# Scores ahead of the turned probabilities: an order change in the attention turns of a two-layer decoder trunk

## The chip, the cores and the metric

The kernel runs on one core of a Trainium2 chip. The metric is the device time of one execution in microseconds (us): the median of three runs is 1085.81 us, the runs lie between 1085.67 and 1086.09. One further execution was recorded by the profiler; all rows below come from it.

The engines are TensorE (PE: matmuls and transposes), VectorE (DVE), ScalarE (ACT), GpSimd (POOL), and SyncE (SP), which only issues transfers. Each runs its own instructions strictly in the order written and waits on semaphores.

## The reference

The input is 512 tokens of width 1024. Two layers follow each other. The first has sliding-window attention with a sink, the second picks 128 keys per query by an indexer and attends to those; both have 16 query heads on 4 key heads of width 64, and both are followed by a squared-ReLU MLP. Cut to what matters here, per block of 128 queries:

```
scores = einsum(q, k) * HEAD_DIM ** -0.5       # one 128-row block of queries
scores = where(valid, scores, -inf)            # window, causal or top-k mask
p = exp(scores - max)                          # softmax, in layer 0 with a sink term
probs = p / sum
out = einsum(probs, v)                         # sums over keys
x = x + rmsnorm(out @ w_out)
```

## The kernel before, in words

All engine streams are written out by hand. Products with the large weights are made as three float32r matmuls (high by high, low by high, high by low); that is the `three`/`dense` pattern of lines 1975 to 1987, called fill below when it stands inside the attention.

The attention of a layer is cut into 16 turns. A turn is one block of 128 queries for four heads. Its work goes through the engines in this order: TensorE makes the scores (`scores`, line 2104: matmuls on 64 rows of the array, two row halves side by side); VectorE masks and scales them into `probs` and finds the maximum (`masked`, line 1435); ScalarE takes the exponential (`expo`, line 1031); VectorE the reciprocal of the sum (line 1442); GpSimd normalises (`normed`, line 779); TensorE transposes each 128x128 block of the probabilities (`transposes`, line 2159, here "turnings": four full-array matmuls against the identity per key block); ScalarE copies the turned block out of its bank (`pt_copy`, line 1038); and TensorE multiplies it with the values (`weighted`, line 2173, here "sums": they write 64 columns of the array at a time).

The turns are pipelined on TensorE. In step n of the loop in `attention` it turns the probabilities of turn n-1, makes the scores of turn n+1, sums turn n-2, turns queries or a new x if the tables `Q_TURN` and `H_TURN` say so (`queries_turned`, line 2084; `new_x`, line 2070), and then does the fill of that step (table `FILL`). Step 9 of the first layer and steps 2 and 5 of the second have no fill. A turn has one or two key blocks in the first layer and one to four in the second. Where the next turn is wider than 256 keys its scores come in two parts, the second behind half of the fill; turnings beyond two blocks also stand there.

What the first instruction of each group waits for:
- scores of turn n+1: the masks of turn n (`s_masked`), because both use the same two banks;
- turnings of turn n-1: the normalised probabilities (`p_done`), and the bank: all turnings, of probabilities, queries and x, go alternately through two banks, and a bank is free when its last user has been copied out (`t_free`);
- sums of turn n-2: the copies (`pt_out`), made a step earlier;
- fill: split weights, and the banks that ScalarE or VectorE has emptied.

ScalarE's stream has in each step: copies of the turned blocks, a half of a weight split in some steps, the high half of turned queries, the exponentials of the next turn, scaled queries or squares of the output, and weight splits. VectorE's has masks, low halves of turned queries, and in the second layer the rounds of the top-k search between all these.

Of the kernel before, what the change touches and what calls it, by code (L numbers as in the profile page):

```python
# [122 lines left out]
TURNS = 16  # L123
# [4 lines left out]
def turn(layer, n):  # L128
    p, i = PAIRS[layer][n // 2]
    return p, i, n % 2  # L130
# [12 lines left out]
def pt_of(layer, n):  # L143
    return range(PT_AT[16 * layer + n], PT_AT[16 * layer + n + 1])
# [34 lines left out]
def q_no(layer, c, j):  # L179


    return 4 * (c - 1) + j if not layer else 7 + 4 * c + j
# [73 lines left out]
def hybrid_trunk(nc, x, x_turned, positions, gains, gains_turned, w_up, w_down, a_in, a_out, sinks, b_in, b_out, consts, out):  # L256
# [4 lines left out]
    with ctx:  # L261
# [305 lines left out]
        def width(layer, i):  # L567
            return len(key_blocks(layer, i)) * P
# [1355 lines left out]
        def _(pe):  # L1924
# [83 lines left out]
            def in_work(layer, s, ks=(0, 1, 2, 3)):  # L2008
                c, h, j = in_step(layer, s)
                u = U[f"in{layer}"] + 2 * c + h  # L2010
                if j == 0 and ks[0] == 0:
                    pe.wait_ge(*low_of(u))
                if c == 0:
                    pe.wait_ge(h_lo, h_no(2 * layer, j, h) + 1)
                ins = dense(u, h, layer, d_no(layer, "in", c, j), in_reg(layer), j, ks)
                if ks[-1] < 3:
                    return
                if h:
                    ins.then_inc(d_done, 1)
                elif j == 3:  # L2020
                    ins.then_inc(first_half_done, 1)
# [24 lines left out]
            def out_work(layer, j, c, h, ks=(0, 1, 2, 3)):  # L2046
                u = U[f"out{layer}"] + 2 * c + h
                if ks[0] == 0:
                    if j == 0:
                        pe.wait_ge(*low_of(u))  # L2050
                    if h == 0 and c == 0:
                        pe.wait_ge(o_lo_done, 8 * layer + max(pair_of(layer, p, j) for p in range(2)) + 1)
                ins = dense(u, h, layer, d_no(layer, "out", c, j), q_reg(layer), j, ks)
                if ks[-1] < 3:
                    return
                if h:
                    ins.then_inc(d_done, 1)
                elif j == 3:
                    ins.then_inc(first_half_done, 1)

            def new_x(norm, j):

                layer = norm // 2
                pe.wait_ge(x_new, 8 * (norm - 1) + 2 * j + 2)
                for h in range(2):
                    bank = t_free(layer, ("h", norm, j, h))
                    if norm == 2 and j == 0:
                        pe.wait_ge(tile_out, LAYER_TILES - 4)
                    for k in range(4):
                        ins = nc.tensor.transpose(bank[:, blk(k)], X[:, j, blk(4 * h + k)], ident[:, 0:P])  # L2070
                    ins.then_inc(h_t, 1)
# [8 lines left out]
            def queries_turned(layer, qn):  # L2080
                bank = t_free(layer, ("q", qn))
                pe.wait_ge(q_roped, qn + 1)
                for r in range(4):
                    ins = nc.tensor.transpose(bank[:, blk(r)], qs[:, qn % 2, blk(r)], ident[:, 0:P])
                ins.then_inc(q_t, 1)
# [42 lines left out]
            def scores(layer, n, rr):  # L2128
                N = 16 * layer + n
                p, i, rh = turn(layer, n)  # L2130
                W, k0 = width(layer, i), key_blocks(layer, i)[0] * P
                if rr == 0:
                    pe.wait_ge(k_lo_done, 4 * layer + i + 1)
                    pe.wait_ge(q_lo_done, q_no(layer, p + 1, i) + 1)
                    if N:
                        pe.wait_ge(s_masked, 4 * N)
                    else:
                        pe.wait_ge(kv_out, 4)
                elif W > 256:
                    pe.wait_ge(s_masked, 4 * N + 2)  # L2140
                qh, ql = q_reg(layer)
                c0 = 256 * rr if W <= 256 else 0
                pairs = []
                for a in range(2):
                    rows = slice(64 * a, 64 * a + 64)
                    t = 4 * p + 2 * rh + rr
                    pairs.append((banks[s_bank(layer, a)][:, c0:c0 + W], qh[rows, t, blk(i)], ql[rows, t, blk(i)],
                                  k_hi[rows, p, k0:k0 + W], k_lo[rows, p, k0:k0 + W]))
                for ins in by_rows(pairs):
                    ins.then_inc(s_ready, 1)  # L2150

            def transposes(layer, n, c):
                N = 16 * layer + n
                K = PT_AT[N] + c
                bank = t_free(layer, ("pt", K))
                if c == 0:
                    pe.wait_ge(p_done, 4 * N + 4)
                for e in range(4):
                    ins = nc.tensor.transpose(bank[:, blk(e)], probs[:, N % 3, e, blk(c)], ident[:, 0:P])
                ins.then_inc(pt_ready, 1)  # L2160
# [17 lines left out]
            def attention(layer):  # L2178
                norm = 2 * layer + 1

                def fill(s, ks=(0, 1, 2, 3)):
                    if s < FILL_OUT[layer]:
                        in_work(layer, FILL_IN[layer] + s, ks)
                    else:
                        m = s - FILL_OUT[layer]
                        out_work(layer, m // 4, m % 4 // 2, m % 2, ks)

                def turned(n):
                    for c, j in Q_TURN[layer].get(n, ()):
                        queries_turned(layer, q_no(layer, c, j))  # L2190
                    for j in H_TURN[layer].get(n, ()):
                        new_x(norm, j)

                def scores_of(n):
                    scores(layer, n, 0)
                    if width(layer, turn(layer, n)[1]) <= 256:
                        scores(layer, n, 1)

                for n in (-1, 0):
                    steps = FILL[layer].get(n, ())  # L2200
                    for s in steps[:1]:
                        fill(s)
                    if n == -1:
                        turned(n)
                        for s in steps[1:]:
                            fill(s)
                    scores_of(n + 1)
                    if n == 0:
                        turned(n)
                        for s in steps[1:]:  # L2210
                            fill(s)
                for n in range(1, TURNS + 2):
                    turning = len(pt_of(layer, n - 1)) if n - 1 < TURNS else 0
                    summing = len(pt_of(layer, n - 2)) if n >= 2 else 0
                    wide = n + 1 < TURNS and width(layer, turn(layer, n + 1)[1]) > 256
                    second = wide or turning > 2 or summing > 2
                    for c in range(min(turning, 2)):
                        transposes(layer, n - 1, c)
                    if n + 1 < TURNS:
                        scores_of(n + 1)  # L2220
                    for c in range(min(summing, 2)):
                        weighted(layer, n - 2, c)
                    turned(n)
                    steps = FILL[layer].get(n, ())
                    for s in steps[:-1]:
                        fill(s)
                    if steps:
                        fill(steps[-1], (0, 1) if second else (0, 1, 2, 3))
                    if second:
                        for c in range(2, turning):  # L2230
                            transposes(layer, n - 1, c)
                        if wide:
                            scores(layer, n + 1, 1)
                        for c in range(2, summing):
                            weighted(layer, n - 2, c)
                        if steps:
                            fill(steps[-1], (2, 3))
# [142 lines left out]
            for s in range(8, 12):  # L2380
                in_work(0, s)
                keys_turned(0, s - 8)
            attention(0)
            out_tail(0)
            mlp(0)
# [37 lines left out]
            for s in range(8, 20):  # L2423
# [5 lines left out]
                if s in (16, 17):  # L2429
                    queries_turned(1, s - 3)  # L2430
            pe.wait_ge(idx_relu, 24)
            attention(1)
            out_tail(1)
            mlp(1)
# [36 lines left out]
```

## Time and profile before

| what | us |
|---|---|
| median of three runs | 1085.81 |
| profiled execution | 1088.47 |
| its span, first to last instruction | 1086.7 |
| TensorE busy | 1055.2 (97%) |
| VectorE busy | 744.4 (68%) |
| ScalarE busy | 540.4 (50%) |
| GpSimd busy | 184.7 (17%) |

The profiled execution took 1088.47 us, of which 1.8 us lie outside its span; it is 2.7 us longer than the median of the runs. TensorE is busy 97% of the span. The attention of the first layer runs from about 55 to 165 us of the span, that of the second from about 611 to 728 us. Start times in rows are us from the start of the span. A matmul's recorded length overlaps that of the next, so the time that TensorE gives to a group is read from the start of its first to the start of the next group's first.

### The profile page before, as it was taken

Reading aid. Unit: us, or ns where it says so; the run is one execution under the profiler, and the core shown is the slowest. Engines: PE = TensorE matmul, PEld = TensorE weight load, DVE = VectorE, ACT = ScalarE, POOL = GpSimd, SP = SyncE. Lnnn points to the kernel's source line nnn. Section 1 sums busy time; section 2 is a strip of 40 time slices with the busy share of each in tenths; the row PEclk is TensorE's granted clock in tenths of the full one; section 3 lists DMA queues with packets and bytes.
Section 4 is the critical chain, followed back from the end, with each engine's and each line's share of the span. In section 5 each row is a group of like instructions: output and inputs, shape, how many; then the busy total and the mean of one; then the engine's idle time right before and its main releaser. Section 6 shows DMA issues by size and latency. Waiting matters only on the chain. (4 is left out here: it accounts for less than half of the span.)

```text
span 1086.7 us, 14782 instructions
## 1 busy us (share of the span) xinstructions
PE 1055.2 (97%) x5372; PEld 856.3 (79%) x5372; DVE 744.4 (68%) x1283; ACT 540.4 (50%) x1018; POOL 184.7 (17%) x330
## 2 busy tenths in 40 slices
PE   7899999999999999999999989999999999999997
PEld 6677678988888888888777766679888888888885
DVE  4364644587698697687678898536586697696684
ACT  6486753454445444425554576645353453453431
POOL 1345420000000000005412377430000000000004
PEclk9899999999999999999999999999999999999999
DMA  9431505634454455432523333005644535535502
GB/s 293 117 79 40 118 1 114 139 78 109 85 114 110 87 114 111 86 78 50 117 59 78 78 77 80 1 1 119 134 92 102 111 84 116 110 84 117 110 8 78
DMA packets 52009, 99.94 MB, mean 92 GB/s; under 512 B 4704, under 2 KB 4832, under 8 KB 51936
## 3 DMA queue, kind: packets, MB, share of 16 engines
q1 hardware_dynamic: 51360, 98.87, 40.4%
q8 instruction: 43, 0.70, 0.3%
q14 instruction: 30, 0.25, 0.1%
q10 hardware_dynamic: 576, 0.11, 0.1%
HBM read 96.88 MB, written 2.10 MB: 91 GB/s over the span
## 5 line engine op out<-in xcount | busy, mean ns | idle before, releaser
L1975 PE MATMUL bank<-r_hi,w_hi 128*128 128x512 f32 (+1 forms) x456 | 177.5, 389 | 0.0
L1976 PE MATMUL bank<-r_hi,w_lo 128*128 128x512 f32 (+1 forms) x456 | 177.4, 389 | 0.0
L1977 PE MATMUL bank<-r_lo,w_hi 128*128 128x512 f32 (+1 forms) x456 | 177.4, 389 | 0.0
L1583 DVE TENSOR_TENSOR w_lo<-w_raw,w_hi 128x1024 fp32r<-128x1024 f32 x84 | 102.1, 1223 | 70.5 <-ACT w_hi L1123 70.4
L1123 ACT ACTIVATE w_hi<-w_raw 128x1024 fp32r<-128x1024 f32 x84 | 87.9, 1056 | 119.5 <-PE bank L1977 82.9
L2314 PE MATMUL bank<-w_hi,hid_hi 128*128 128x512 f32 x336 | 130.7, 389 | 0.0
L2315 PE MATMUL bank<-w_lo,hid_hi 128*128 128x512 f32 x336 | 130.7, 389 | 0.0
L2316 PE MATMUL bank<-w_hi,hid_lo 128*128 128x512 f32 x336 | 130.7, 389 | 0.0
L1132 ACT ACTIVATE w_hi<-w_raw,gT 128x512 fp32r<-128x512 f32 x96 | 64.5, 716 | 106.5 <-DMA w_raw<-in_w_mlp_up 75.1
L787 POOL TENSOR_TENSOR acc<-acc,G 128x512 f32<-128x512 f32 x8 | 13.0, 1650 | 594.3 <-ACT waste L983 594.3
L1977 PEld LDWEIGHTS bank<-r_lo,w_hi 128*128 128x128 f32 (+1 forms) x456 | 85.2, 187 | 18.2
L1975 PEld LDWEIGHTS bank<-r_hi,w_hi 128*128 128x128 f32 (+1 forms) x456 | 85.2, 187 | 18.0
L1976 PEld LDWEIGHTS bank<-r_hi,w_lo 128*128 128x128 f32 (+1 forms) x456 | 85.2, 187 | 18.0
L779 POOL TENSOR_TENSOR probs<-probs,small 128x256 f32<-128x256 f32 (+3 forms) x128 | 78.1, 641 | 89.6 <-DVE small L1442 89.4
L1985 PE MATMUL bank<-w_hi,r_hi 128*128 128x512 f32 x208 | 86.5, 416 | 1.4 <-issue 0.6
L1664 DVE SCALAR_TENSOR_TENSOR w_lo<-w_raw,gT,w_hi 128x512 fp32r<-128x512 f32 x96 | 68.3, 747 | 27.6 <-ACT w_hi L1132 27.6
L1987 PE MATMUL bank<-w_hi,r_lo 128*128 128x512 f32 x208 | 82.0, 394 | 0.0
L1986 PE MATMUL bank<-w_lo,r_hi 128*128 128x512 f32 x208 | 81.6, 392 | 0.0
L1031 ACT ACTIVATE probs<-probs,small 128x257 f32<-128x257 f32 (+5 forms) x128 | 65.4, 516 | 25.1 <-DVE small L1435 25.0
L2315 PEld LDWEIGHTS bank<-w_lo,hid_hi 128*128 128x128 f32 x336 | 63.1, 188 | 13.1
L2316 PEld LDWEIGHTS bank<-w_hi,hid_lo 128*128 128x128 f32 x336 | 63.1, 188 | 13.1
L2314 PEld LDWEIGHTS bank<-w_hi,hid_hi 128*128 128x128 f32 x336 | 63.1, 188 | 13.1
(200 smaller groups left out, 2143.1 us busy)
## 6 DMA issues: line engine op xcount, KB each, us to landing
w_raw<-in_w_mlp_up SPq DMA_DIRECT2D x64, 512.0 KB, 6.5
w_raw<-in_w_mlp_down SPq DMA_DIRECT2D x64, 512.0 KB, 6.9
w_raw<-in_b_w_in SPq DMA_DIRECT2D x16, 512.0 KB, 6.9
w_raw<-in_a_w_in SPq DMA_DIRECT2D x8, 512.0 KB, 8.7
w_raw<-in_a_w_out SPq DMA_DIRECT2D x8, 512.0 KB, 5.7
w_raw<-in_b_w_out SPq DMA_DIRECT2D x8, 512.0 KB, 6.6
xt<-in_x_turned SPq DMA_DIRECT2D x8, 256.0 KB, 6.3
w_raw<-in_a_w_in SPq DMA_DIRECT2D x8, 256.0 KB, 6.5
```

The source lines that it names most:

```text
L779: nc.gpsimd.tensor_tensor(v, v, inv_sum[:, N % 3, c:c + 1].to_broadcast([P, W]), ALU.mult).then_inc(p_done, 1)
L1123: nc.scalar.activation(half_of(w_hi[:, u % 2, :], a), b_of(name, a), ACT.Copy).then_inc(b_hi_done, 1)
L1583: nc.vector.tensor_tensor(half_of(w_lo[:, u % 2, :], a), b_of(PRODUCTS[i][1], a), half_of(w_hi[:, u % 2, :], a).bitcast(f32), ALU.subtract ...
L1975: nc.tensor.matmul(bank, whi, xhi, start=start, stop=False)
L1976: nc.tensor.matmul(bank, wlo, xhi, start=False, stop=False)
L1977: return nc.tensor.matmul(bank, whi, xlo, start=False, stop=stop)
L1985: nc.tensor.matmul(bank[:], xh, hi[:, k, :], start=h == 0 and k == 0, stop=False)
L1986: nc.tensor.matmul(bank[:], xh, lo[:, k, :], start=False, stop=False)
L1987: ins = nc.tensor.matmul(bank[:], xl, hi[:, k, :], start=False, stop=h == 1 and k == 3)
L2314: nc.tensor.matmul(bank[:], xh[:, k, blk(j)], hi[:, k, :], start=k == 0, stop=False)
L2315: nc.tensor.matmul(bank[:], xh[:, k, blk(j)], lo[:, k, :], start=False, stop=False)
L2316: ins = nc.tensor.matmul(bank[:], xl[:, k, blk(j)], hi[:, k, :], start=False, stop=k == 3)
```

## The change

In each step n from 1 to 14 the scores of turn n+1 are issued ahead of the first two blocks' turnings of turn n-1; before, they stood behind them. Step 15 and later have no scores. Nothing is added or removed, and the streams of the other four engines are the same.

```
--- before.py
+++ after.py
@@ -2214,10 +2214,10 @@
                     summing = len(pt_of(layer, n - 2)) if n >= 2 else 0
                     wide = n + 1 < TURNS and width(layer, turn(layer, n + 1)[1]) > 256
                     second = wide or turning > 2 or summing > 2
+                    if n + 1 < TURNS:
+                        scores_of(n + 1)
                     for c in range(min(turning, 2)):
                         transposes(layer, n - 1, c)
-                    if n + 1 < TURNS:
-                        scores_of(n + 1)
                     for c in range(min(summing, 2)):
                         weighted(layer, n - 2, c)
                     turned(n)
```

TensorE, first layer, step 6, before: the end of the last fill (`w_hi`, `r_lo`), the turnings of two key blocks (`probs`), the scores of turn 7 (`k_hi`, `k_lo`), the sums (`pt`) and four query turnings (`qs`).

```order
L1987 MATMUL bank<-w_hi,r_lo 128x512
L2159 MATMUL bank<-ident,probs 128x128 x8
L2104 MATMUL bank<-k_hi,r_hi 128x128 x2
L2104 MATMUL bank<-k_hi,r_lo 128x128 x2
L2104 MATMUL bank<-k_lo,r_hi 128x128 x2
L2104 MATMUL bank<-k_hi,r_hi 128x128 x2
L2104 MATMUL bank<-k_hi,r_lo 128x128 x2
L2104 MATMUL bank<-k_lo,r_hi 128x128 x2
L2173 MATMUL bank<-pt,kvs 64x256 x4
L2084 MATMUL bank<-ident,qs 128x128 x4
```

The same place of TensorE with the change:

```order
L1987 MATMUL bank<-w_hi,r_lo 128x512
L2104 MATMUL bank<-k_hi,r_hi 128x128 x2
L2104 MATMUL bank<-k_hi,r_lo 128x128 x2
L2104 MATMUL bank<-k_lo,r_hi 128x128 x2
L2104 MATMUL bank<-k_hi,r_hi 128x128 x2
L2104 MATMUL bank<-k_hi,r_lo 128x128 x2
L2104 MATMUL bank<-k_lo,r_hi 128x128 x2
L2159 MATMUL bank<-ident,probs 128x128 x8
L2173 MATMUL bank<-pt,kvs 64x256 x4
L2084 MATMUL bank<-ident,qs 128x128 x4
```

The eight turnings moved from ahead of the twelve score matmuls to behind them, next to the sums.

TensorE, second layer, steps 5 and 6, as a difference: there is no fill between the steps, so the turnings of turn 5 (the row with the minus) followed the query turnings of step 5 at once.

```order
 L2104 MATMUL bank<-k_lo,r_hi 128x256 x2
+L2159 MATMUL bank<-ident,probs 128x128 x8
 L2173 MATMUL bank<-pt,kvs 64x256 x2
 L2084 MATMUL bank<-ident,qs 128x128 x4
-L2159 MATMUL bank<-ident,probs 128x128 x8
 L2104 MATMUL bank<-k_hi,r_hi 128x256 x2
 L2104 MATMUL bank<-k_hi,r_lo 128x256 x2
```

The row with the plus is turn 4's, moved behind the scores of turn 6. With the change the scores of turn 7 follow the query turnings.

## Rows read from the trace of the kernel before

**Rows 1.** Windows: length; busy PE, PEld, DVE, ACT, POOL; granted clock; DMA
```profile
55.00:165.00 110.00, 106.83 (x712) 82.27 (x711) 59.40 (x185) 74.27 (x204) 47.42 (x104) 1.00 0.25 58
611.00:728.00 117.00, 109.15 (x717) 76.47 (x716) 82.95 (x243) 78.20 (x205) 64.66 (x91) 0.99 0.17 38
628.00:631.00 3.00, 3.00 (x9) 2.27 (x8) 2.93 (x12) 1.44 (x6) 3.00 (x7) 0.50 0.01 3
```

**Rows 2.** TensorE's timeline, first layer, step 4 (start, length, instruction, idle before)
```profile
78.35 0.39 PE L1987 MATMUL bank<-w_hi,r_lo 128*128 128x512 f32 x1
78.59 1.03 PE L2159 MATMUL bank<-ident,probs 128*128 128x128 f32 x8
79.55 0.39 PE L2104 MATMUL bank<-k_hi,r_hi 64*128 64x256 f32 x2
...
80.45 1.08 PE L2173 MATMUL bank<-pt,kvs 128*64 128x256 f32 x8
```

**Rows 3.** TensorE's timeline, places that price a change of kind
```profile
59.31 0.39 PE L1987 MATMUL bank<-w_hi,r_lo 128*128 128x512 f32 x1
59.63 0.33 PE L2104 MATMUL bank<-k_hi,r_hi 64*128 64x128 f32 x2
...
63.29 0.60 PE L2159 MATMUL bank<-ident,probs 128*128 128x128 f32 x4
63.82 0.39 PE L2104 MATMUL bank<-k_hi,r_hi 64*128 64x256 f32 x2
...
64.73 0.66 PE L2084 MATMUL bank<-ident,qs 128*128 128x128 f32 x4
65.14 0.48 PE L1985 MATMUL bank<-w_hi,r_hi 128*128 128x512 f32 x1
...
590.01 0.60 PE L2084 MATMUL bank<-ident,qs 128*128 128x128 f32 x4
590.37 0.48 PE L1985 MATMUL bank<-w_hi,r_hi 128*128 128x512 f32 x1
```

**Rows 4.** A turning and its first copy, TensorE and ScalarE, step 3
```profile
73.26 1.03 PE L2159 MATMUL bank<-ident,probs 128*128 128x128 f32 x8
...
73.89 1.09 ACT L1038 ACTIVATE pt<-bank 128x512 f32<-128x512 f32 x2 [0.32 <-PE bank L2159]
```

**Rows 5.** First layer, steps 9 and 10, TensorE and ScalarE
```profile
107.62 1.03 PE L2159 MATMUL bank<-ident,probs 128*128 128x128 f32 x8
...
108.41 1.07 ACT L1038 ACTIVATE pt<-bank 128x512 f32<-128x512 f32 x2
...
115.21 0.66 PE L2084 MATMUL bank<-ident,qs 128*128 128x128 f32 x4 [1.62 <-ACT pt L1038]
```

**Rows 6.** Second layer, step 3, TensorE, and VectorE's last mask before it
```profile
625.67 0.63 PE L2159 MATMUL bank<-ident,probs 128*128 128x128 f32 x4 [1.69 <-POOL probs L779]
626.44 0.38 PE L2104 MATMUL bank<-k_hi,r_hi 64*128 64x256 f32 x2
...
625.93 0.35 DVE L1435 CUSTOM_DVE_ANT_0 probs<-bank,band,small 128x128 f32<-128x128 f32 x1
```

**Rows 7.** Second layer, steps 5 to 8, TensorE and ScalarE
```profile
637.24 1.03 PE L2159 MATMUL bank<-ident,probs 128*128 128x128 f32 x8
...
638.97 1.07 ACT L1038 ACTIVATE pt<-bank 128x512 f32<-128x512 f32 x2
...
642.25 0.66 PE L2159 MATMUL bank<-ident,probs 128*128 128x128 f32 x4 [1.47 <-DVE r_lo L1376]
...
645.40 0.66 PE L2084 MATMUL bank<-ident,qs 128*128 128x128 f32 x4 [0.56 <-ACT pt L1038]
...
662.97 0.45 PE L2104 MATMUL bank<-k_hi,r_hi 64*128 64x384 f32 x2 [1.73 <-DVE small L1435]
```

**Rows 8.** Second layer, step 9, VectorE and TensorE
```profile
664.89 0.61 DVE L1435 CUSTOM_DVE_ANT_0 probs<-bank,score,small 128x384 f32<-128x384 f32 x1
...
665.19 1.04 PE L2159 MATMUL bank<-ident,probs 128*128 128x128 f32 x8
```

More of the change, by code:

```diff
@@ L2216, in attention @@
                     second = wide or turning > 2 or summing > 2
+                    if n + 1 < TURNS:
+                        scores_of(n + 1)
                     for c in range(min(turning, 2)):
                         transposes(layer, n - 1, c)
-                    if n + 1 < TURNS:
-                        scores_of(n + 1)
                     for c in range(min(summing, 2)):
```

## The prediction, made before the changed kernel was run

> **What bounds the kernel.** I read the table of busy time first: TensorE is busy 97% of the span, so what counts is the time that TensorE gives to its groups, and its waits. Then the windows over the two attentions [rows 1]: TensorE is busy 106.83 of 110 us in the first and 109.15 of 117 us in the second. There are 3.2 and 7.9 us of idle time, and nothing else in the kernel is touched by the change. VectorE (83.0 us) and ScalarE (78.2 us) are far from full in the second, but both work in a fixed order, so a late item delays what stands behind it. Last I read the timelines of TensorE at each wait, with the engine that ended it.
>
> No work is added. The sum has two kinds of terms: what another order of matmul kinds costs TensorE, and what each wait becomes.
>
> **Changes of kind.** Fill and turnings use the whole array, scores use it in two row halves, sums in two column halves. In a usual step before [rows 2] the last fill starts at 78.35, turnings follow 0.24 later, scores 0.96 after those (eight turnings), sums 0.90 after those: 2.10 us from the last fill to the sums. In the new order: fill to scores takes 0.32 (59.31 to 59.63) [rows 3]; scores to the next whole-array group 0.91 (63.82 to 64.73) [rows 3]; then the turnings, up to a group of another kind, 0.96 as before [rows 2]; and four turnings that stand behind scores take 0.41 where four behind fill take 0.36 [rows 3], so 0.05 more. Sum 2.24, that is about 0.15 us more per step. It is one more change of kind: fill, turnings | scores | sums | fill has three, fill | scores | turnings | sums | fill has four. Turnings followed by sums have no row here; I take them like turnings followed by scores, 0.53 for four (63.29 to 63.82) [rows 3]. If that change were free the term would be 0.06, if it cost twice as much 0.24.
>
> The Trainium skill, page "TensorEngine Tiling (Array Packing)", section "Key Properties", says that changing the tiling mode drains TensorE. It gives no price. By that rule alone the new order has one drain more in each step, which speaks against the change; whoever counts matmuls alone finds nothing.
>
> Of the 14 steps of a layer that have scores, step 1 has no sums and as many changes as before. So 13 steps, 26 in both layers: 3.9 us if TensorE never waited. The waits alter this, layer by layer.
>
> **First layer.** Steps 2 to 8 add 7 x 0.15 = 1.05, of which step 8 gives back about 0.15, since its query turning waits for GpSimd, whose work follows the fill. So TensorE reaches step 9 about 0.9 late. There the turnings started at 107.62 and ScalarE's copies at 108.41 [rows 5]. In the new order they start at 107.62 + 0.9 + 0.08 (fill to scores instead of turnings) + 0.91 (scores) = 109.51. A copy can begin 0.63 after the first turning (73.26 to 73.89, where ScalarE stood idle for it) [rows 4], with the 0.05 above 0.68: 110.19, that is 1.78 us later than 108.41. From that copy on ScalarE has no gap before (half a weight split, four exponentials, the output's high half, another split) until the copy which the query turnings of step 10 wait for; they start at 115.21 after 1.62 idle [rows 5]. All of it moves by 1.78, so these start at about 116.99. TensorE's own lateness is hidden in that wait; 0.8 us come on top. The copy that sets it is late because it now stands behind scores. Step 11's 0.15 is given back at a wait for split weights that hang on the same ScalarE chain. Steps 12 to 14 add 0.45. First layer: 1.78 + 0.45 = 2.2 us. In the other query steps (2, 4, 6) the copy had over 1.4 us in hand, and the new order takes about 1.0.
>
> **Second layer.** Here VectorE's top-k rounds set the pace of the masks. In step 3 TensorE waited 1.69 us for the probabilities, turned them (625.67) and started the scores at 626.44; the last mask began at 625.93 and took 0.35, so it ended at 626.28 [rows 6]. The scores can't go earlier, since the masks hang on VectorE's rounds and not on TensorE. In the new order TensorE waits for the masks, starts the scores at 626.44 as before, and the four turnings that lay inside the wait stand behind them: 0.53 + 0.05 = 0.58 us late [rows 3]. This replaces what steps 1 to 3 would add; in steps 1 and 2 the same happens on a smaller scale and is hidden at 626.44.
>
> Steps 4 and 5 add 0.15 each. Step 5's turnings start at 637.24 + 0.73 + 0.08 + 0.91 = 638.96, and their copy at 639.64 instead of 638.97 [rows 7]: 0.7 late. From there ScalarE goes without a gap to the high half of the queries, VectorE then makes the low half, and this ended the 1.47 us before the second block's turnings at 642.25 [rows 7]. In step 6 the scores now fill that wait. So TensorE would gain up to 0.9 us, but it gains nothing: ScalarE's chain, 0.7 late, goes on to the copy that releases the query turnings at 645.40, and VectorE's chain to the masks that release the second part of the scores at 662.97 after 1.73 us idle [rows 7]. Both move by 0.7. What TensorE wins in between it waits there. At 662.97 the second layer is 0.7 late.
>
> In step 9 the turnings started at 665.19; the last mask began at 664.89 and took 0.61, so it ended at 665.50 [rows 8]. The scores, now first, are ready at 665.19 + 0.7 + 0.08 = 665.97 but must wait for the masks at 665.50 + 0.7 plus a few hundredths, 666.25. That costs 0.28 besides the 0.15: 1.1 late. Step 10's 0.15 goes into a wait of 0.5 for the output's low half. Steps 11 to 14 add 0.6: 1.7 us.
>
> **Sum.** 2.2 + 1.7 = 3.9 us. The profiled execution of 1088.47 would become 1092.4. It lies 2.7 above the median of the runs, and I carry the difference over: 1085.8 + 3.9 = 1089.7 us. That the sum equals 26 x 0.15 is chance: waits give some back and two chains add.
>
> **Rivals.**
> 1. Scores fill the waits of the turnings, and it gets faster. The waits ended by probabilities, or by the bank of a query turning, are 1.69, 1.47 and two of 0.41 and 0.25. Scores (0.9) in their place would save 0.9 + 0.9 + 0.41 + 0.25 = 2.5 us; with masks 0.9 earlier, up to 0.9 of the 1.73 at 662.97 too. With free changes of kind the time is 1082.4 to 1083.3, with 3.9 for them still 1086.3. It decides as soon as a turn's masks are done when the turnings would have started. Against it: at 626.44 the scores were released by the masks and not by the turnings [rows 6], and the wait at 662.97 ends with VectorE's rounds.
> 2. Nothing: changes of kind are hidden by weight loads and the chains have more slack than I read. 1085.8, with one chain late 1086.6. Against it are the two pairs 0.24 / 0.32 and 0.36 / 0.41 [rows 2, 3].
> 3. The clock. From 628 to 631 TensorE had half its clock, 1.2 GHz instead of 2.4 (0.50) [rows 1], after the idle time of step 3; the fill there took about twice its time, so such a stretch of 3 us costs some 1.5 us. The new order makes single waits longer: about 2.1 us in step 3 and some 2.4 us ahead of the query turnings of step 10 in the first layer, where 1.62 left the clock alone. One such stretch more gives 1091.2. If the one in the second layer fell where TensorE waits anyway, 1088.2.
>
> That the order does not change can be left out: the streams show it.
>
> **How the numbers follow.** Of this kernel a difference of about 0.2%, 2.2 us, can be told from none. Forecast as worked out: 0.63, 1087.9 to 1091.0 by itself (changes of kind at 0.08 a step below, a chain later by a us above). Rival 3 with a slower clock: 0.17. Rival 2: 0.13. Rival 1: 0.07, of which I put 0.04 at faster and the rest within 0.2%. Slower by over 0.2% (over 1088.0) holds most of the first and all of the slower clock: 0.80. Within 0.2%: 0.16. Faster: 0.04. The range that leaves out 2 in 10 is 1086.9 to 1091.7.
>
> **What would show it right or wrong.** In the trace after, scores follow fill by 0.32 and turnings follow scores with a first step longer by 0.05; from the last fill to the sums 2.24 instead of 2.10. The query turnings of step 10 in the first layer still wait for ScalarE's copy and start near 117.0. The scores of step 3 in the second layer start no earlier than before, and the turnings behind them. TensorE's idle time in both windows changes by under 1.5 us, though its work takes longer. I am wrong if fill to sums takes 2.1, if the wait at 662.97 shrinks, or if the masks run ahead of TensorE in steps 1 to 9 of the second layer.

## The result and the profile after

The changed kernel takes 1090.31 us (median of 11 executions, 1086.6 to 1092.5); the kernel before, on the same chip, takes 1085.67 us (11 executions). The ratio is 1.0042 with a 95% interval of 1.0029 to 1.0054, that is 3.1 to 5.9 us slower. The profiled execution took 1090.9 us, its span 1089.1 us.

Spans of the two profiles differ by 2.4 us only, because they differ by 2.5 us of the other sign before the change begins. In the start-up, at about 34 us, TensorE waited 4.60 us for VectorE and then ran at half clock for 6.8 us in the profile of before, against 3.25 and 3.4 us in that of after. So I compare start times with those of the same instruction before, and count from the first attention's fill (56.71 before, 54.22 after). By that measure the first layer costs 3.7 us and the second 1.2.

The windows of after (length; busy PE, PEld, DVE, ACT, POOL; granted clock; DMA), to be held against [rows 1]:

```profile
55.00:165.00 110.00, 106.49 (x688) 79.56 (x687) 58.50 (x181) 72.25 (x201) 47.50 (x104) 0.98 0.26 58
611.00:728.00 117.00, 110.59 (x705) 76.11 (x705) 83.98 (x246) 78.08 (x204) 65.83 (x94) 0.97 0.18 40
116.00:119.00 3.00, 3.00 (x9) 2.33 (x8) 2.65 (x2) 2.27 (x9) 0.00 (x0) 0.50 0.98 203
628.00:631.00 3.00, 3.00 (x19) 1.80 (x16) 2.86 (x10) 1.16 (x4) 3.00 (x7) 0.50 0.02 5
648.50:651.50 3.00, 2.98 (x7) 2.42 (x8) 2.90 (x11) 1.60 (x7) 3.00 (x5) 0.50 0.67 177
```

TensorE's idle time has hardly changed (3.5 us of 110 instead of 3.2; 6.4 of 117 instead of 7.9). The first layer has a stretch at half clock (0.50, so 1.2 GHz) that it did not have before, at 116. The second has a further one at 648.5.

A usual step, TensorE, first layer, step 4 of after, against [rows 2]:

```profile
76.13 0.39 PE L1987 MATMUL bank<-w_hi,r_lo 128*128 128x512 f32 x1
76.45 0.38 PE L2104 MATMUL bank<-k_hi,r_hi 64*128 64x256 f32 x2
...
77.35 1.09 PE L2159 MATMUL bank<-ident,probs 128*128 128x128 f32 x8
78.37 1.08 PE L2173 MATMUL bank<-pt,kvs 128*64 128x256 f32 x8
```

Fill to scores takes 0.32, scores to turnings 0.90, turnings to sums 1.02: 2.24 us from the last fill to the sums, where it was 2.10. From the fill of one step to that of the next, steps 3, 5 and 7 each add 0.13 to 0.16.

Steps 9 and 10 of the first layer, TensorE and then ScalarE, against [rows 5]:

```profile
106.95 1.09 PE L2159 MATMUL bank<-ident,probs 128*128 128x128 f32 x8
109.05 0.39 PE L2104 MATMUL bank<-k_hi,r_hi 64*128 64x256 f32 x2 [0.42 <-DVE small L1435]
114.45 0.66 PE L2084 MATMUL bank<-ident,qs 128*128 128x128 f32 x4 [2.38 <-ACT pt L1038]
```

```profile
107.64 1.08 ACT L1038 ACTIVATE pt<-bank 128x512 f32<-128x512 f32 x2 [0.80 <-PE bank L2159]
108.61 1.92 ACT L930 ACTIVATE w_hi<-w_raw 128x2048 fp32r<-128x2048 f32 x1
113.81 1.08 ACT L1038 ACTIVATE pt<-bank 128x512 f32<-128x512 f32 x2
```

With the 2.49 us added by which after is ahead, the turnings of step 9 start at 109.44, their copies at 110.13 (1.72 later than before) and the query turnings at 116.94 (1.73 later), behind a wait of 2.38 instead of 1.62. ScalarE now stands idle for TensorE at 107.64. The 0.42 at 109.05 is new: scores of turn 11 wait for the masks of turn 10, whose scores went out only 3.00 us earlier.

The second layer of after, first TensorE against [rows 6] and [rows 7], then ScalarE:

```profile
627.60 0.41 PE L2104 MATMUL bank<-k_hi,r_hi 64*128 64x256 f32 x2 [1.87 <-DVE small L1435]
644.09 0.66 PE L2159 MATMUL bank<-ident,probs 128*128 128x128 f32 x4 [0.27 <-DVE r_lo L1376]
647.23 0.66 PE L2084 MATMUL bank<-ident,qs 128*128 128x128 f32 x4 [1.47 <-ACT pt L1038]
664.23 0.44 PE L2104 MATMUL bank<-k_hi,r_hi 64*128 64x384 f32 x2 [0.24 <-DVE small L1435]
666.92 0.44 PE L2104 MATMUL bank<-k_hi,r_hi 64*128 64x384 f32 x2 [0.31 <-DVE small L1435]
```

```profile
640.80 1.08 ACT L1038 ACTIVATE pt<-bank 128x512 f32<-128x512 f32 x2
646.57 1.09 ACT L1038 ACTIVATE pt<-bank 128x512 f32<-128x512 f32 x2
655.25 1.06 ACT L914 ACTIVATE r_hi<-w_raw 128x1024 fp32r<-128x1024 f32 x1 [2.67 <-DMA w_raw<-in_b_w_out]
```

This layer begins 1.16 us later on its profile's time scale than before, which is the 3.65 us that the first layer left less the 2.49. The scores of step 3 are 1.16 late too, so the change has not moved them by itself. The query turnings are 1.83 late (0.67 more), and their wait has grown from 0.56 to 1.47 while that of the second block's turnings shrank from 1.47 to 0.27: most of what was won in the one was waited in the other. At 664.23 (662.97 before) it is 1.26, so 0.10 more than at the start and not the 0.7 forecast, and the wait there shrank from 1.73 to 0.24. At the layer's end it is 2.39.

### The profile page after: what moved, and what is told of

Its sections match the earlier page's. It is cut to its first block and busy times, and to the rows that moved or that the text cites. A ratio compares the mean times of both kernels' runs of the same rounds, so it can differ in the third digit from the quotient of the medians.

```text
span 1089.1 us, 14782 instructions
## 1 busy us (share of the span) xinstructions
PE 1059.9 (97%) x5372; PEld 856.0 (79%) x5372; DVE 743.9 (68%) x1283; ACT 541.4 (50%) x1018; POOL 185.0 (17%) x330
```

## The experiments

Each changes `attention`; where a condition is named, the steps outside it keep the order of before:

```
first = <condition>
if first and n + 1 < TURNS:
    scores_of(n + 1)
for c in range(min(turning, 2)):
    transposes(layer, n - 1, c)
if not first and n + 1 < TURNS:
    scores_of(n + 1)
```

**The first layer alone.** `first = layer == 0`.

> The scores stand first in the steps of the first layer alone. Kinds and chains: 26 changes of kind are halved (13 x 0.15 = 2.0 us), and the copies of step 9 come 1.8 us late, so the query turnings of step 10 start 1.8 later than before measured from the start of the attention, and the first layer ends 2.1 us later; the second layer adds nothing. Time +2.1 us against the kernel before, or +3.7 where a stretch at half clock follows the longer wait of step 10. Kinds alone, without chains: query turnings of step 10 no later than before, +0.5 from the steps after them. Second layer as the only cause: 0.

Measured: ratio 1.0019 (1.0007 to 1.0031). In its profile the query turnings of step 10 are 1.73 late behind a wait of 2.38, a half-clock stretch follows, and the layer ends 3.7 late. The second layer, unchanged, returned 0.75 of it; the table below says why.

**The second layer alone.** `first = layer == 1`.

> The scores stand first in the steps of the second layer alone. Kinds and chains: first layer as before with 1.62 us of wait in step 10; scores of steps 1 to 3 of the second layer at the same distance as before, sums 0.6 later, query turnings of step 6 0.7 later; the layer ends 1.2 us later (as in the profile of the change) to 1.8 us later (if the weight load between steps 6 and 8 takes as long as before). Time +1.2 to +1.8 us. Kinds alone: +2.0 from 13 steps. The clock as the only cause: 0.

Measured: 1.0007 (0.9997 to 1.0017), which can't be told from no change. In the profile the first layer is as before and the second costs 1.22, as it does in after. The ratios of the two halves add up to 1.0026, with the one for both at 1.0042. With intervals of 0.001 to each side these times don't contradict a plain sum, but they don't show one closely either.

**Step 9 of the first layer alone.** `first = (layer, n) == (0, 9)`. Is it the late copy that sets the query turnings of step 10?

> The scores stand first in step 9 of the first layer and nowhere else. Chain theory: step 9's turnings start 1.0 later, the copies 0.9 later (108.41 becomes 109.3), and the query turnings of step 10 start 0.9 later, though TensorE idles before them: +0.9 us, a bit less where the wait for split weights gives back. Rival, only changes of kind cost: 0.15 go into the wait of 1.62 us: 0.0 us.

TensorE and then ScalarE in that kernel, which is 2.37 us ahead of before at this place:

```profile
106.27 1.09 PE L2159 MATMUL bank<-ident,probs 128*128 128x128 f32 x8
113.76 0.66 PE L2084 MATMUL bank<-ident,qs 128*128 128x128 f32 x4 [2.74 <-ACT pt L1038]
```

```profile
106.96 1.09 ACT L1038 ACTIVATE pt<-bank 128x512 f32<-128x512 f32 x2 [0.80 <-PE bank L2159]
113.12 1.08 ACT L1038 ACTIVATE pt<-bank 128x512 f32<-128x512 f32 x2
```

The copies are 0.92 late, the query turnings 0.92, and 0.93 is what is left at the layer's end. The chain through ScalarE is shown: one step's order, with no work added and TensorE idle behind it, costs its whole delay. The ratio is 1.0007 (0.9994 to 1.0020), too wide to tell 0.9 us by itself: this rests on the profile. The wait of 2.74 was followed by no half-clock stretch.

**All but that step.** `first = (layer, n) != (0, 9)`.

> The change as it is, but step 9 of the first layer keeps the old order. Chain theory: TensorE comes to step 9 0.9 us late, the turnings and the copies are 0.9 late (not 1.8), so the query turnings of step 10 start 0.9 later than before, with a wait of about 1.6 us as before and so without a stretch at half clock behind it; the first layer ends 0.9 + 0.45 = 1.35 later instead of 2.15. Time about 0.8 us below the changed kernel, 2.4 below where that one has the half clock. Kinds alone: 0.15 below the changed kernel.

TensorE at steps 9 and 10:

```profile
110.83 0.39 PE L2104 MATMUL bank<-k_hi,r_hi 64*128 64x256 f32 x2 [1.45 <-DVE small L1435]
...
114.45 0.66 PE L2084 MATMUL bank<-ident,qs 128*128 128x128 f32 x4 [0.60 <-ACT pt L1038]
```

The query turnings are 0.83 late, what steps 2 to 8 had gathered, and the layer ends 1.15 late. That is 0.9 less than the 2.05 of the changed kernel where its clock holds (its third profile, below), and 2.5 less than the 3.7 where it doesn't. I had expected a wait of 1.6 ahead of the query turnings; it is 0.60, because the waiting moved to the scores (1.45, for masks), which changes nothing in the sum. Ratio 1.0014 (1.0003 to 1.0026).

**Three changes of kind instead of four.** Scores, sums, turnings: the turned block is summed a step later anyway, so the sums may stand between.

```
 if n + 1 < TURNS:
     scores_of(n + 1)
+for c in range(min(summing, 2)):
+    weighted(layer, n - 2, c)
 for c in range(min(turning, 2)):
     transposes(layer, n - 1, c)
-for c in range(min(summing, 2)):
-    weighted(layer, n - 2, c)
```

> Order scores, sums, turnings, so there are three changes of kind as before (fill | scores | sums | turnings, fill), with scores still first and turnings later by the sums as well. If the 0.15 us per step is the price of the fourth change, a step without query turnings (step 3, 5 or 7 of the first layer) takes as long from fill to fill as before. The copies come another 0.6 to 1.1 us later than with the change: the query turnings of step 10 in the first layer start 2.3 to 2.8 us later than before less the 0.9 that the kinds cost there, and those of steps 4 and 6 now follow turnings at once and wait 0.3 us for a copy. Time +2 to +3 us in all. If scores first is what costs and not the change of kind, steps 3, 5, 7 are 0.15 longer and time is over +4 us.

TensorE in step 4 and, last, the query turnings of step 10:

```profile
76.00 0.39 PE L1987 MATMUL bank<-w_hi,r_lo 128*128 128x512 f32 x1
76.31 0.38 PE L2104 MATMUL bank<-k_hi,r_hi 64*128 64x256 f32 x2
...
77.22 1.08 PE L2173 MATMUL bank<-pt,kvs 128*64 128x256 f32 x8
78.23 1.09 PE L2159 MATMUL bank<-ident,probs 128*128 128x128 f32 x8
...
115.35 0.66 PE L2084 MATMUL bank<-ident,qs 128*128 128x128 f32 x4 [2.96 <-ACT pt L1038]
```

From the fill of one step to the next, steps 3, 5 and 7 now take 0.02 to 0.05 less than before: the 0.15 is gone with the fourth change of kind, though the scores still stand first. So it is the price of the change of kind. The Trainium skill says in "TensorEngine Tiling (Array Packing)", "Key Properties", that changing the tiling mode drains TensorE. The traces agree as far as they go: they show a cost, 0.15 us for one change more per step, and not the drain itself.

For the total the expectation of 2 to 3 us missed by far: ratio 1.0067 (1.0055 to 1.0079), some 7 us. The turnings now stand 1.0 us further back still, so the copies and all that hangs on them come later: 2.39 at step 10, 6.3 at the end of the first layer. Of the 3.9 in between, 1.6 is a half-clock stretch, 0.7 a longer wait for split weights in step 11 (1.26 us instead of 0.60), and 0.5 to 0.7 falls on each of three steps behind it in which TensorE now waits for ScalarE's copies (0.34, 0.34 and 0.25 us). The expectation had only the waits of steps 4 and 6 in it.

**The wait filled in the second layer.** `first = (layer, n) == (1, 6)`. Does the wait of 1.47 us that the scores fill there bring anything?

> The scores stand first in step 6 of the second layer and nowhere else: the one place where they can fill a wait of the turnings (1.47 us for the bank of a query turning). Chain theory: scores 0.5 us or more earlier, the wait at the second block's turnings shrinks from 1.47 to about 0.5 us, the sums start 0.8 to 0.9 earlier, and the query turnings still start where ScalarE's copy ends, with 1.4 us of wait in place of 0.56; gain 0.0 us at the end of the layer. Rival 1 (filling waits pays): 0.9 us faster.

The query turnings (that kernel is 2.06 ahead there, before step 6 and here):

```profile
643.34 0.66 PE L2084 MATMUL bank<-ident,qs 128*128 128x128 f32 x4 [1.17 <-ACT pt L1038]
```

The sums came 0.60 earlier, the query turnings not at all (0.00): the gain is given back 2.2 us later at the next wait, for the same copy of ScalarE. Ratio 0.9991 (0.9980 to 1.0002), which can't be told from no change.

**ScalarE's chain ahead of step 10 shortened**, in either order. Half a weight split of unit 8 (0.95 us, L914) is moved behind the copies that the query turnings wait for:

```
+                        if u in COPY_AHEAD:        # COPY_AHEAD = (8,)
+                            split_half(u, 0)       # behind the copies
                         if u in HALVED:
                             split_half(u, 1)
...
+                        if u in COPY_AHEAD:        # where it stood
+                            continue
```

> The kernel before, with one item of ScalarE moved: the first half of the split of weight unit 8 stands behind the two copies of step 10 of the first layer instead of ahead of them. If the query turnings of step 10 hang on ScalarE's chain and on nothing else, they start 0.96 us earlier and their wait shrinks from 1.62 to 0.66 us; the split ends when it ended, so nothing else is later: -0.9 us. If the wait for that split (0.6 us, two fills later) is what counts, it grows by what was won and the gain is 0 to 0.3 us.

> The same move in the changed kernel. Query turnings of step 10 start 0.96 earlier than in the changed kernel, 0.8 later than before; wait 1.4 in place of 2.38 us, and no stretch at half clock behind it. -0.9 us against the changed kernel, or -2.5 where that one has the stretch; but if the wait for the split takes the gain, 0 to -0.3, or -1.9 with the clock.

The query turnings of step 10 in the old order (that profile is 0.14 behind before), and in the new one (1.47 ahead); line numbers are shifted by a few:

```profile
114.38 0.66 PE L2089 MATMUL bank<-ident,qs 128*128 128x128 f32 x4 [0.68 <-ACT pt L1039]
```

```profile
114.53 0.66 PE L2089 MATMUL bank<-ident,qs 128*128 128x128 f32 x4 [1.44 <-ACT pt L1039]
```

They start 0.97 and 0.94 earlier than without the move, which is the half split's 0.95, and keep it to the layer's end: 0.97 earlier than before in the old order, 1.11 late in the new. Between the two orders the first layer still differs by 2.1 us. So ScalarE's chain, not TensorE's work, sets this place in both. Neither profile has a half-clock stretch in the attentions. The ratios are 0.9990 (0.9978 to 1.0002) and 1.0009 (0.9994 to 1.0024). By its ratio the new order with the move lies 3.6 us below the changed kernel. That is more than the 0.9 to 2.5 expected, but the two intervals together allow some 2 us either way. The old order with the move has the lowest ratio of all, but isn't provably faster than before.

**The same two kernels again**, to see what belongs to the order and what to the execution.

> The changed kernel, unaltered, looked at a second time. It asks whether the stretch at half clock behind the query turnings of step 10 in the first layer belongs to this kernel. If the half clock follows the wait there, it comes again within 2 us of the turnings, which start behind a wait of 2.3 to 2.5 us, and costs 1.5 to 1.6 us again. If it comes and goes by itself, it is somewhere else or absent. The wait itself, and the turnings 1.7 to 1.8 us behind the base (the first attention's start), repeat in either case. In the second layer ScalarE's half split of the output weights starts between 7.3 and 8.1 us after the issue of their transfer; if late, near 8.0, the wait for the masks late in step 8 ends 0.6 to 0.7 us late.

> The changed kernel a third time, with the same expectation as for its second look.

> The kernel before, unaltered, looked at a second time. If half clock follows long waits alone, there is none at step 10 of the first layer (wait 1.6 us), and one after the wait of step 3 in the second layer. ScalarE's half split of the output weights in the second layer starts between 7.3 and 8.1 us after the issue of their transfer; the first look had 8.05. If 7.4 comes here too, the spread belongs to the transfer and not to the kernel.

Their single times are 1091.63, 1090.45 and 1086.61 us. A window and the query turnings of step 10, of the changed kernel's second profile, then of its third:

```profile
116.40:119.80 3.40, 3.40 (x9) 2.67 (x9) 2.35 (x4) 3.15 (x10) 0.36 (x2) 0.50 1.07 243
```

```profile
115.73 0.65 PE L2084 MATMUL bank<-ident,qs 128*128 128x128 f32 x4 [2.38 <-ACT pt L1038]
```

```profile
116.40:119.80 3.40, 3.31 (x17) 2.81 (x18) 2.35 (x8) 3.40 (x11) 1.13 (x3) 1.00 0.95 226
```

```profile
116.49 0.66 PE L2084 MATMUL bank<-ident,qs 128*128 128x128 f32 x4 [2.39 <-ACT pt L1038]
```

The turnings are 1.74 and 1.73 late, the wait is the same, but the clock is 0.50 in one and 1.00 in the other: the fill behind the turnings loses 1.6 us or nothing, and the first layer costs 3.7 or 2.05. Of the four profiles with this wait of 2.38 (three of the changed kernel, one of the first layer alone) three have the stretch. So has the one with 2.96 (sums between), but not the one with 2.74 (step 9 alone). None of the four with this step in the old order, behind 1.62 or 1.63 us, has it.

## Where the second layer's time goes

I had taken every difference there for the change's. The transfer of the output weights, though, ends one wait in all profiles. ScalarE's split of it, and the scores late in step 8, in before, in the changed kernel's third profile, and in the new order with the split moved (L914 and L2104 are L915 and L2109 there), one fence each:

```profile
653.99 1.06 ACT L914 ACTIVATE r_hi<-w_raw 128x1024 fp32r<-128x1024 f32 x1 [3.25 <-DMA w_raw<-in_b_w_out]
```

```profile
654.81 1.06 ACT L914 ACTIVATE r_hi<-w_raw 128x1024 fp32r<-128x1024 f32 x1 [2.61 <-DMA w_raw<-in_b_w_out]
```

```profile
663.80 0.44 PE L2104 MATMUL bank<-k_hi,r_hi 64*128 64x384 f32 x2 [0.56 <-DVE small L1435]
```

```profile
652.07 1.06 ACT L915 ACTIVATE r_hi<-w_raw 128x1024 fp32r<-128x1024 f32 x1 [2.52 <-DMA w_raw<-in_b_w_out]
```

```profile
661.06 0.45 PE L2109 MATMUL bank<-k_hi,r_hi 64*128 64x384 f32 x2 [0.47 <-DVE small L1440]
```

From the split to the scores it is 8.98 us in before (653.99 to 662.97 in [rows 7]), and 8.99 in both others: the wait at 662.97 hangs on the transfer. What matters is when SyncE issues it and how long it takes. All profiles with an unmixed second layer, in us, shifts against before and counted from the layer's start:

| kernel | order | half clock behind | issue | issue to split | scores at 662.97 | from there to the end | layer |
|---|---|---|---|---|---|---|---|
| before | old | step 3 | 0 | 8.05 | 0 | 0 | 0 |
| before, again | old | step 3 | -0.02 | 7.68 | -0.39 | 0.00 | -0.39 |
| first layer alone | old | step 3 | -0.03 | 7.34 | -0.73 | -0.02 | -0.75 |
| step 9 alone | old | step 3, sooner | -0.24 | 7.83 | -0.46 | +0.02 | -0.44 |
| split moved | old | none | -0.86 | 7.82 | -1.08 | -0.01 | -1.09 |
| after | new | steps 3, 6 | +0.68 | 7.47 | +0.10 | +1.13 | +1.23 |
| second layer alone | new | steps 3, 6 | +0.69 | 7.48 | +0.13 | +1.09 | +1.22 |
| after, second | new | step 1 | -0.13 | 7.77 | -0.40 | +1.08 | +0.68 |
| after, third | new | step 1 | -0.17 | 7.41 | -0.80 | +1.11 | +0.31 |
| all but step 9 | new | step 1 | -0.18 | 7.32 | -0.90 | +1.08 | +0.18 |
| split moved | new | none | -0.83 | 7.31 | -1.56 | +1.10 | -0.46 |

The shift of the scores is that of the issue plus the transfer's difference from 8.05, to 0.02 us, in each row. Behind it the new order costs 1.08 to 1.13 in all six, and the old one nothing. Ahead of it the order costs 0.7 where a half-clock stretch lies on the fill behind step 3 (+0.68 against 0), and nothing where there is no stretch at all (-0.83 against -0.86); each of these stands on one kind of profile, and for a stretch behind step 1 there is none in the old order to compare with. The mean of the six new rows is 0.53, of the five old ones -0.53.

The wait at this place is shorter in each new row (none in one, 0.24 to 0.93 us in the others) than in any old one (1.03 to 1.73). In the pair without a stretch, the new order above waits 0.47, and the old order:

```profile
661.08 0.44 PE L2109 MATMUL bank<-k_hi,r_hi 64*128 64x384 f32 x2 [1.52 <-DVE small L1440]
```

Counted from the layer's start these scores go out 0.48 us apart, and the waits differ by 1.05. So TensorE arrives 0.57 us later in the new order; that much of its extra time is hidden in this wait. The other 0.48 comes from the transfer (7.31 against 7.82).

## Why the prediction came out right

I forecast 1089.7 us, that is 3.9 more, likely between 1086.9 and 1091.7. Measured are 4.6 more, 3.1 to 5.9. The steps of the first layer held; one of the second layer was 0.6 too high, and something that the forecast has no term for made up for it. By its steps:

- **The change of kind**, 0.15 a step: right. 2.24 us from fill to sums, 0.13 to 0.16 per step, and with three changes none of it.
- **Step 9 to step 10 of the first layer**, 1.78: right in mechanism and size (1.73). Step 9 alone gives 0.92 of it, the steps ahead 0.83, the sum of both 1.75.
- **First layer**, 2.2: 2.05 where the clock holds. What rose above it is the rival of the slower clock, and at the place that I named for it (1.6 us behind the query turnings of step 10). I gave it 0.17; it came in three of four profiles. In these it was no alternative to the forecast but an addition to it. Whether the chance was mis-sized for the timed executions isn't shown, as said below.
- **Second layer, step 3**: right. The scores go no earlier (+0.00), the wait is 1.87, masks end it.
- **The gain of step 6 given back**: right, shown by that step alone.
- **The chain of 0.7 to the scores at 662.97**: this step failed in part. Its 0.7 reached the query turnings (0.67) and the issue of the transfer (0.68), and where the transfer took 8.05 in before it took 7.47 in after, so 0.10 was left. And with no half-clock stretch the 0.7 isn't there (-0.83 against -0.86). I took the stretch behind step 3 in the profile of before for a fixed part of the kernel. It makes TensorE late in steps 4 and 5; in the old order without it, TensorE reaches the query turnings of step 5 early enough to wait 0.54 us for ScalarE's copy.
- **My own sign of being wrong** came: the wait at 662.97 shrank, from 1.73 to 0.24 in after. I had named it for the rival of the filled waits, whose masks would come sooner. They didn't, beyond the spread of the transfer; TensorE came later. The sign was badly chosen, since a chain that moves by less than TensorE does shortens the wait too.
- **Behind it**, 0.28 and 0.15 and 0.6, so 1.0: 1.1.

The sum that the profiles give without a stretch in the first layer is 2.05 there and 1.06 in the second (0.53 less -0.53): 3.1 us, at the lower end of 3.1 to 5.9. If three of four executions had the stretch, as the profiles do, 1.2 would be added: 4.3 us.

The timed executions don't bear that out as it stands. Their mean granted clocks are on record, and in the profiled ones this mean goes with the number of half-clock stretches of 3.4 us, the start-up's 6.8 counted as two: 0.997 with one, 0.995 with two, 0.993 or 0.994 with three, 0.992 with four. The 11 executions of the changed kernel lie at 0.9946 on average, and 64 of the kernel before, from the later comparisons, at 0.9943. So no more half clock shows in the changed kernel on the whole. Three quarters of a stretch would lower its mean by 0.0012 (3.4 us at half clock are 0.0016 of the span); with a spread of 0.0018 among the 11 that speaks against so much more, without ruling out some. Three of its 11 executions have 0.997, as the one profile has in which the start-up's stretch is the only one. At like clocks it is slower all the same: 1089.4 against 1086.2 us at 0.995 (medians of 3 and 18), 1092.1 against 1087.9 at 0.993 (3 and 18), on different chips. What a stretch costs hangs on where it lies, and the timed executions don't show where.

So the 3.9 has the right size in part by luck: 0.6 too much in the second layer was made up by something else. The profiles name the clock for it; the timed executions don't confirm that, so it stays open. The rival of the filled waits fell at once: the waits of the turnings went (1.69, 1.47) and came back at the next wait on the same ScalarE or VectorE chain (1.87, 1.47). That of no effect is outside the interval.

Left open: why a wait of 2.38 is followed by half clock in three profiles and not in the fourth, and the one of 2.74 isn't either. How many of the timed executions have the stretch at step 10 isn't known.

## What to carry to other kernels

Putting other work into a wait is worth nothing if the work pushed back feeds the engine that ends the next wait. Ask of each moved group what copies it out and what that copy stands ahead of: 0.9 us of scores ahead of eight transposes cost 0.92 us some seven microseconds later, with TensorE idle in between. On an engine with array tilings, count the changes of tiling in each order first: here one more cost 0.15 us in each step in which TensorE didn't wait. And before pricing a chain from one profile, look at a second one of the same kernel: a slow stretch or a late transfer in the only trace makes a chain look tight that isn't.

## What the runs showed of the hardware that was not expected

Stretches at half clock (1.2 instead of 2.4 GHz) come and go between executions of the same program. In the second attention they start at 627.8 and 648.3 in one profile of the changed kernel, and at 621.6 and 620.3, alone, in the others; the one behind step 10 of the first layer costs 1.6 us, while the one at 648.3 made its fill 1.1 us longer than in the third profile and left the scores at 662.97 where the transfer put them. The start-up's lasted 3.4 us in ten of the 13 profiles and 6.8 in three. The transfer of the output weights, issued in the same surroundings, took 7.31 to 8.05 us until ScalarE could start on it; that alone moves the end of this kernel by up to 0.7 us.
